# The expert stage of a decoder layer as dense matmuls over both whole tables, in place of row fetches

## The chip, the cores and the metric

The kernel runs on one core of one Trainium2 chip. The metric is the device time of one execution in microseconds; the median of three runs of the kernel before is 2040.55 us (2039.8 to 2042.72).

## The reference

One layer of a decoder, on 512 prompt tokens and 32 sample tokens (8 sequences of 4), D = 1024, everything in f32. First a mixer: RMSNorm, one input projection, a gMLP part and an attention part with three dilated windows (12 heads of 64; the samples attend to a cache of keys and values), then an output projection added to x. Then the expert part ("PEER"), which this case is about:

```python
def block(xb):                                    # xb: RMSNorm of x, tokens x 1024
    q = (xb @ w_q).reshape(TOK_BLK, PEER_HEADS, 2, DK_HALF)          # 8 heads, 2 halves of 128
    s = jnp.einsum('thcd,hcnd->thcn', q, sub_keys)                   # 128 scores for each half
    s1, i1 = lax.top_k(s[:, :, 0], TOPK)                             # the best 16 of each half
    s2, i2 = lax.top_k(s[:, :, 1], TOPK)
    cand = s1[..., :, None] + s2[..., None, :]                       # 16 x 16 sums
    cid = i1[..., :, None] * N_KEYS + i2[..., None, :]               # expert number, 0 to 16383
    top_s, pos = lax.top_k(cand, TOPK)
    eid = take_along_axis(cid, pos)
    g = softmax(top_s)
    hid = gelu(einsum('thkd,td->thk', u_tab[eid], xb))
    return einsum('thk,thkd->td', g * hid, v_tab[eid])
```

So each token selects 8 x 16 = 128 of 16384 experts. Each expert has a row of 1024 in `u_tab` and one in `v_tab`, 67.1 MB a table. The result is added to x, and a last RMSNorm gives y. The gates and the hidden values are per token and expert; the sum over a token's 128 experts is all that leaves the stage.

## The kernel before

Tokens lie in five tiles: four of 128 prompt tokens and one of the 32 samples (`TILES`, lines 39 to 41). The program is written out engine by engine: each of `block.sync`, `block.tensor`, `block.scalar`, `block.vector` and `block.gpsimd` is one list of instructions that runs in order, and semaphores tie the lists together. A wait therefore holds back all that stands behind it in its list.

**Up to the expert stage** (lines 317 to 604; to about 354 us). Norm and transposes, the input projection (`L474`, stationary: 128 columns of the normed x, moving: 384 or 512 columns of weights), attention (`L506` to `L564`; for the samples three pairs of heads work side by side in column strips of 32, `L517`), and the output projection (`project_out`, `L593`; the sample tile in strips, `L598`).

**Scoring.** For each head and tile, `queries` (`L622`) multiplies 128 tokens (stationary) with 256 columns of w_q (moving), `turn_queries` transposes the result, and `key_scores` (`L641`) gives 2 x 128 scores. ScalarE copies each result out of PSUM (`copy`, `L718`).

**Routing.** `route` (`L1112` to `L1167`) finds, on VectorE, the 16 best of each half, the 256 sums, the 16 best of these, and from their positions the expert numbers (one-hot compare `L1152`, product `L1156`, sum `L1160`, then two instructions that make the number and write it to `eid`). It is a chain of 13 links, each waiting for the one before. `finish_gates` makes the softmax.

**The experts.** A step is one head of one tile: 16 slots. For each slot, GpSimd fetches, by an indirect DMA (`L1339`), one row of `u_tab` for each of 128 tokens: 128 x 4 KB. `dots` (`L1223`) multiplies them with x on VectorE and sums. ScalarE takes the Gelu (`L870`), VectorE multiplies with the gates (`weights`, `L1229`), ScalarE makes for each slot a diagonal matrix of the 128 weights (`L877`), and `slot` (`L651`) multiplies it with the 128 fetched rows of `v_tab`, two matmuls of 512 columns, adding into one PSUM sum of the tile. The 32 samples are spread over 128 partitions, four slots at a time, so their eight heads take two steps. That makes 34 steps x 16 = 544 slots. The rings hold 8 rows blocks for `u_tab` and 4 for `v_tab` (`UR`, `VR`, line 64). Routing of the next tile's heads is spread over the steps of the tile before. The end is `copy` of the sum, a square, a root and `finish_y` (`L1207`).

Of the kernel before, what the change touches and what calls it, by code (L numbers as in the profile page):

```python
# [14 lines left out]
P = 128  # L28
# [35 lines left out]
UR, VR = 8, 4  # L64


GROUPS = P // NSAMP
LINKS = 13
STEPS = [HEADS] * (NT - 1) + [HEADS // GROUPS]
FIRST = [sum(STEPS[:t]) for t in range(NT)]  # L70
NSTEP = sum(STEPS)


def build(nc, x_p, x_s, k_cache, v_cache, gains, w_in, ln_gb, w_sT, b_sT, w_out, w_q, keysT, u_tab, v_tab,
          ident_c, logc_c, smask_c, snew_c, rope_c, iota_c, tril_c, blockm_c,
          y_p, y_s, k_p, v_p, k_s, v_s, gv_s):
    ctx = ExitStack()
    with ctx:
# [8 lines left out]
        area_w = sb("area_w", 16384)  # L87
        area_r = sb("area_r", 14720)
        area_t = sb("area_t", KD * TOK)
        area_x = sb("area_x", NT * D)  # L90
        area_v = sb("area_v", 6400)
# [22 lines left out]
        u_ring = [cut(area_r, s * D, D) for s in range(UR)]  # L114
        v_ring = [cut(area_r, (UR + s) * D, D) for s in range(VR)]
        keys = cut(area_r, (UR + VR) * D, 2 * HEADS * NKEYS)
# [15 lines left out]
        h_stage = [cut(area_v, s * D, D) for s in range(2)]  # L132
        v_tok = cut(area_v, 0, NT, DB)
        u_tok = cut(area_v, NT * DB, NT, DA)
        vn = cut(area_v, NT * (DB + DA), NT, DA)
        xn = cut(area_v, 0, NT, D)
# [16 lines left out]
        iota = sb("iota", TOPK)  # L153
# [4 lines left out]

        eid = sb("eid", NSTEP * TOPK, U32)
        gate = sb("gate", NSTEP * TOPK)  # L160
        hid = sb("hid", TOPK)
        gelu = sb("gelu", TOPK)
        wts = sb("wts", TOPK)
        ident4 = sb("ident4", NSAMP)

        diag = [cut(area_c, s * P, P) for s in range(VR)]
        q_row = cut(area_c, 512, 2 * P)
        q_col = cut(area_c, 768, 2, P)
        s_cur = [cut(area_v, NT * D + a, 2, NKEYS) for a in (0, 1024)]
        s_left = cut(area_v, NT * D + 256, 2, NKEYS)  # L170
        cand = cut(area_c, 1024, TOPK * TOPK)
        cand_left = cut(area_c, 1280, TOPK * TOPK)
        hot = [cut(area_v, NT * D + 512 + c * 256, TOPK, TOPK) for c in range(2)]
        tops = cut(area_c, 1536, HEADS, TOPK)
        eid_samp = cut(area_c, 1664, SLOTS)
        gate_samp = cut(area_c, 1792, SLOTS)
        rt = cut(area_c, 1920, 9 * TOPK)
        rtu = sb("rtu", 5 * TOPK, U32)
        val = [rt[:, c * TOPK:(c + 1) * TOPK] for c in range(2)]
        idf = [rt[:, (2 + c) * TOPK:(3 + c) * TOPK] for c in range(2)]  # L180
        pick = [rt[:, (4 + c) * TOPK:(5 + c) * TOPK] for c in range(2)]
        top = rt[:, 6 * TOPK:7 * TOPK]
        den8 = rt[:, 7 * TOPK:7 * TOPK + 8]
        rden8 = rt[:, 7 * TOPK + 8:8 * TOPK]
        eidf = rt[:, 8 * TOPK:9 * TOPK]
        idx = [rtu[:, c * TOPK:(c + 1) * TOPK] for c in range(2)]
        pos = rtu[:, 2 * TOPK:3 * TOPK]
        digit = [rtu[:, (3 + c) * TOPK:(4 + c) * TOPK] for c in range(2)]

# [8 lines left out]
        acc = bank[0]  # L198
        x_cur = wide(1, D)
        ps_q, ps_qT, ps_s = half(4), half(5), half(6)  # L200
# [24 lines left out]
        q_done, q_copied, q_turned, qT_copied = sem("q_done"), sem("q_copied"), sem("q_turned"), sem("qT_copied")  # L225
        s_done, s_ready = sem("s_done"), sem("s_ready")
        tops_exped = sem("tops_exped")
        u_landed = [sem(f"u_landed{s}") for s in range(UR)]
        v_landed = [sem(f"v_landed{s}") for s in range(VR)]
        u_free, v_free = sem("u_free"), sem("v_free")  # L230
# [7 lines left out]
        block = ctx.enter_context(nc.Block())  # L238


        N_CONST = 1 + NT + 1 + 2 * NB + 7 + GROUPS
# [1186 lines left out]
```

## Time and profile before

| | |
|---|---|
| median of three runs | 2040.55 us |
| profiled execution, its own time | 2051.2 us |
| its span, first to last instruction | 2048.3 us |
| mean granted TensorE clock | 0.966 of full speed |
| instructions | 19348 |

The profile is of one execution. Busy times are those of instructions that compute; waiting and DMA-issuing instructions are not in them, save that GpSimd's indirect DMAs are (their work on GpSimd is real). The 40 slices of the page are 51.2 us each. PE is TensorE, PEld its weight loads (beside the matmuls), DVE VectorE, ACT ScalarE, POOL GpSimd, SP SyncE, which has the plain loads. In names, `area_w`, `area_r` and so on are pieces of on-chip memory that are used for many things in turn, and `bank` is PSUM.

### The profile page before, as it was taken

The page shows a single profiled execution, that of the slowest core. Times are in us where ns is not written, and L with a number is a line of the kernel's source. Part 1 is how long each engine was busy: PE and PEld are TensorE (multiplying, and loading weights), DVE is VectorE, ACT ScalarE, POOL GpSimd, SP SyncE. Part 2 cuts the span into 40 slices and gives each one's busy share as a digit, 9 for nine tenths or more (in the row PEclk, how much of TensorE's full clock was granted, in tenths as well). Part 3 has the DMA queues.
Part 4 walks back from the last instruction along what each step waited for, and adds up shares of the span by engine and source line. Part 5 has one row for each costly group of instructions (what it writes and reads, how often), then busy time and mean ns, then how long its engine had stood idle before and what let it go on. Part 6 is the DMA issues. An engine that isn't in the chain of part 4 may idle for free.

```text
span 2048.3 us, 19348 instructions
## 1 busy us (share of the span) xinstructions
PE 1625.9 (79%) x5414; PEld 745.2 (36%) x5414; DVE 1147.9 (56%) x3207; ACT 392.8 (19%) x1051; POOL 1057.8 (52%) x1168
## 2 busy tenths in 40 slices
PE   6999888978888877777777778777777777877677
PEld 3566454444443333333333333333322323322211
DVE  2220565467677777656555665666556555666641
ACT  2111443122221111111111211111121111111212
POOL 3000100145565565566666666666666666666663
PEclk9999899999999999999999999999999999999999
DMA  6110875588998898899999999999999999999996
GB/s 214 63 66 9 305 264 190 203 312 309 322 345 335 335 332 336 324 362 369 371 353 358 369 376 368 354 363 367 364 361 374 352 366 367 357 359 358 380 367 240
DMA packets 188136, 640.99 MB, mean 313 GB/s; under 512 B 19408, under 2 KB 35072, under 8 KB 187936
## 3 DMA queue, kind: packets, MB, share of 16 engines
q0 software_dynamic: 160640, 587.53, 77.0%
q1 hardware_dynamic: 27424, 52.60, 7.5%
q8 instruction: 34, 0.56, 0.1%
q14 instruction: 38, 0.31, 0.0%
HBM read 634.44 MB, written 5.60 MB: 312 GB/s over the span
## 4 chain that ended last, share of the span: by engine, by line
PE 34%; DMA 19%; POOL 16%; DVE 13%; issue 12%; another core or an unknown queue 3%; ACT 1%; DVEq 0%; SPq 0%; ACTq 0%; POOLq 0%
POOL area_r L1339 16%; PE bank L651 13%; DMA area_r<-in_v_tab,eid 11%; PE bank L474 8%; DMA area_r<-in_u_tab,eid 7%; PE bank L622 4%; DVE area_r L1223 4%; PE bank L593 3%; PE bank L564 1%; PE bank L412 1%; PE bank L517 1%; DMA area_w<-in_w_in 1%; PE bank L471 1%; DMA area_w<-in_v_cache 1%
## 5 line engine op out<-in xcount | busy, mean ns | idle before, releaser
L651 PE MATMUL bank<-area_r,area_c 128*128 128x512 f32 (+1 forms) x2176 | 1067.6, 623 | 348.8 <-DMA area_r<-in_v_tab,eid 282.6
L1223 DVE CUSTOM_DVE_ANT_0 area_r<-area_r,bank 128x1024 f32<-128x1024 f32 x544 | 640.4, 1218 | 308.5 <-DMA area_r<-in_u_tab,eid 284.8
L651 PEld LDWEIGHTS bank<-area_r,area_c 128*128 128x128 f32 (+1 forms) x2176 | 380.7, 190 | 965.7 <-issue 838.9
L1339 POOL DMA_INDIRECT area_r<-in_v_tab,eid x544 | 514.9, 947 | 399.8 <-PE bank L651 199.5
L1339 POOL DMA_INDIRECT area_r<-in_u_tab,eid x544 | 510.4, 938 | 288.3 <-issue 156.6
L877 ACT ACTIVATE area_c<-ident,wts 128x128 f32<-128x128 f32 (+1 forms) x544 | 197.5, 391 | 557.8 <-PE bank L651 266.4
L474 PE MATMUL bank<-area_w,area_t 128*128 128x384 f32 (+1 forms) x448 | 158.7, 510 | 7.5 <-DMA area_w<-in_w_in 5.9
L622 PE MATMUL bank<-area_w,area_t 128*128 128x256 f32 (+3 forms) x640 | 145.7, 381 | 3.2 <-ACT area_c L718 2.5
L622 PEld LDWEIGHTS bank<-area_w,area_t 128*128 128x128 f32 (+1 forms) x640 | 110.8, 175 | 47.0 <-issue 19.8
L474 PEld LDWEIGHTS bank<-area_w,area_t 128*128 128x128 f32 x448 | 84.4, 192 | 70.0 <-issue 17.5
L1317 POOL MEMSET area_x<- 128x192 f32 x2 | 0.5, 258 | 151.6 <-ACT area_r L718 151.6
L718 ACT ACTIVATE area_v<-bank 128x256 f32<-128x256 f32 (+3 forms) x54 | 20.8, 385 | 268.4 <-remote 96.9
L718 ACT ACTIVATE area_c<-bank 128x256 f32<-128x256 f32 (+1 forms) x80 | 28.8, 360 | 222.5 <-remote 157.8
L718 ACT ACTIVATE area_x<-bank 128x384 f32<-128x384 f32 (+7 forms) x97 | 38.4, 422 | 152.8 <-PE bank L474 76.6
L1035 DVE CUSTOM_DVE_ANT_0 area_x<-bank,area_c 96x640 f32<-96x640 f32 (+4 forms) x64 | 29.1, 492 | 66.6 <-PE bank L506 51.1
L1334 POOL DMA_DIRECT2D area_w<-in_v_cache x8 | 7.0, 879 | 106.6 <-DMA area_w<-in_k_cache 56.2
L593 PE MATMUL bank<-area_w,area_t 128*128 128x512 f32 x128 | 55.3, 593 | 1.2 <-issue 1.2
L870 ACT ACTIVATE gelu<-hid 128x16 f32<-128x16 f32 x34 | 7.3, 215 | 242.6 <-issue 191.7
L1134 DVE MAX8 area_c<-area_c 128x8 f32<-128x256 f32 (+1 forms) x40 | 17.0, 426 | 61.3 <-remote 44.0
L996 DVE TENSOR_TENSOR rope_ab<-area_x,rope 128x96 f32<-128x96 f32 (+1 forms) x20 | 5.1, 256 | 79.3 <-ACT area_x L718 79.3
L1223 DVE DVE_READ_ACCUMULATOR2_ANT hid<- 128x1 f32 x544 | 44.8, 82 | 0.0
L1138 DVE MATCH_VALUE_LOAD rtu<-area_c 128x8 f32 (+1 forms) x40 | 3.6, 90 | 71.0 <-remote 59.7
(136 smaller groups left out, 1058.9 us busy)
## 6 DMA issues: line engine op xcount, KB each, us to landing
area_w<-in_k_cache SPq DMA_DIRECT2D x8, 1920.0 KB, 9.2
area_w<-in_v_cache POOLq DMA_DIRECT2D x8, 1920.0 KB, 9.1
area_w<-in_w_in SPq DMA_DIRECT2D x6, 1536.0 KB, 12.6
area_r<-in_u_tab,eid POOLq DMA_INDIRECT x544
area_r<-in_v_tab,eid POOLq DMA_INDIRECT x544
area_w<-in_w_q SPq DMA_DIRECT2D x8, 1024.0 KB, 10.6
area_x<-in_x_p SPq DMA_DIRECT2D x8, 512.0 KB, 8.9
area_w<-in_w_out SPq DMA_DIRECT2D x1, 4096.0 KB, 14.0
```

The lines of the kernel that those rows point to most:

```text
L412: return pe.transpose(out, src, ident[0:n, 0:n])
L471: mm = pe.matmul(half(u % 3)[CG * g:CG * g + n, 0:m], featT[:, k, a:a + n], w_ring[c % W_SLOTS][:, k, g * m:(g + 1) * m], start=(k == 0), ...
L474: mm = pe.matmul(half(u % 3)[0:n, 0:w], featT[:, k, a:a + n], w_ring[c % W_SLOTS][:, k, 0:w], start=(k == 0), stop=(k == KD - 1))
L517: mm = pe.matmul(wide(u % 2, D)[CG * g:CG * g + CG, lo:hi], q_blk[b % 2][:, pr * CG:(pr + 1) * CG], src[:, pr, :], start=(i == 0), stop=(i ...
L593: mm = pe.matmul(half(c)[0:n, :], featT[:, k, a:a + n], w_o[:, k, c * 512:(c + 1) * 512], start=(k == 0), stop=(k == KD - 1))
L622: mm = pe.matmul(ps_q[0:n, 0:2 * P], featT[:, k, a:a + n], area_w[:, bass.ds(h * WQ + k * 2 * P, 2 * P)], start=(k == 0), stop=(k == KD - 1))
L651: mm = pe.matmul(acc[0:n, c, :], diag[s][:, 0:n], v_ring[s][:, c * 512:(c + 1) * 512], start=False, stop=False, skip_group_check=True)
L718: return nc.scalar.activation(out, src, ACT.Copy, scale=scale)
L877: nc.scalar.activation(diag[j % VR][:, 0:n], eye[:, 0:n], ACT.Copy, scale=wts[:, j:j + 1]).then_inc(diag_ready, 1)
L1035: return vec.tensor_tensor_reduce(out=out, in0=scores, in1=counts, scale=-1.0, scalar=3e38, op0=ALU.add, op1=ALU.min, accum_out=least)
L1223: vec.tensor_tensor_reduce(out=u_ring[s], in0=u_ring[s], in1=x_cur, scale=1.0, scalar=0.0, op0=ALU.mult, op1=ALU.add, accum_out=hid[:, j:j ...
L1339: nc.gpsimd.indirect_dma_start(out=ring[s], out_offset=None, in_=table, in_offset=bass.IndirectOffsetOnAxis(ap=eid[:, column:column + 1], ...
```

## The change

The experts are no longer fetched. The tokens are taken in two groups: 256 (tiles 0 and 1), and 288 (tiles 2 and 3 and the samples). An expert's number is 128 i1 + i2. A step handles the 128 experts with one i2 (all i1); 2 x 128 = 256 steps.

- **Table one** (`table_one`): a block of `u_tab`, transposed on the host, 512 KB, is loaded by SyncE into a ring of four. Eight matmuls, stationary 128 x 128 of the block, moving 256 or 288 tokens of x, give 128 experts x tokens. ScalarE takes the Gelu into a ring of 58 blocks (`mix`); the samples have one of 24.
- **The weight matrix**: for each token, 128 x 128 (i1 by i2), zero where an expert isn't selected. `route` now keeps i1 and i2 apart (12 links, no number made), and writes them and the gates to `slots`. `turn_slots` transposes these, so that a token's 128 slots lie along partitions. For a token, `hots` makes on VectorE two matrices, slots x 128: gate at i1, and 1 at i2. `build_weights` multiplies the two; four tokens (a quad) fill one bank, and ScalarE copies it in strides into a stage of 32 tokens. GpSimd's queue writes each stage of 2 MB to memory (`w_kept`), and SyncE loads it back by blocks of eight i2 (`load_w_block`).
- `mixes` multiplies the Gelu block with the weights of that i2 on VectorE.
- **Table two** (`table_two`): stationary 128 experts x 128 tokens of the mixed block, moving 512 columns of the block of `v_tab`; four matmuls a step, adding in four banks through all 128 steps. For the samples, every fourth step, 8 matmuls with 32 columns of weights, each of four steps in its own strip of 32 partitions of a bank; the four strips are added at the end.
- **Queries** now hold w_q stationary and move 256 or 288 tokens, so their result needs no transpose; the key scores of the second group go to memory (`s_kept`) and are loaded again for its routes. x goes to memory (`x_kept`) while its place holds the stages, and is loaded back.
- Order: 16 heads of scores, then the steps. Routes of the first two tiles stand before the steps, the other 24 between steps 57 and 103; table two of group 0 begins at step 57 and goes in up to two a step; the last 18 of group 1 stand behind the last step. All loops are written out.

The diff, cut to its core:

```diff
+G1 = G2 = 256
+STEPS = 2 * N2
+RING, SRING = 58, 24
+UR, VR = 4, 6
+QUAD = 4
+CHUNK = 32
+BLOCK = 8
+V_FROM = 57
+LAG = 18
+def quads_upto(step):
+    return upto(0, 64, 4, 52, step) if step < 75 else upto(64, QUADS - 64, 75, 131, step)
+SLOTS_AT = {0: 2, 1: 3, 2: 74, 3: 98, 4: 122}
...
 # sync
+            for s in range(STEPS + 1):
+                if s == V_FROM - 8:
+                    sp.wait_ge(route_link, 2 * HEADS * LINKS)
+                    for v in range(VR):
+                        load_v(v)
+                    for b in range(2):
+                        sp.wait_ge(s_stored[b], 16 * HEADS)
+                        sp.wait_ge(w_stored[b], 16 * stored_before(G1 // CHUNK)[b])
+                    load_w_block(0)
+                    load_w_block(1)
+                if s + UR < STEPS:
+                    sp.wait_ge(h_done, s + 1)
+                    load_u(s + UR)
+                for v in v_in(s):
+                    if v + VR < STEPS:
+                        what, value = v_free_for(v + VR)
+                        if what == "tiles":
+                            sp.wait_ge(v_done, value)
+                        else:
+                            sp.wait_ge(samp_done, value)
+                        load_v(v + VR)
...
 # tensor
+            def table_one(s):
+                g, _ = group_of(s)
+                a, n = first_token(g), width(g)
+                pe.wait_ge(u_landed[s % UR], 16 * (s // UR + 1))
+                if s >= 2:
+                    pe.wait_ge(h_read, s - 1)
                 for k in range(KD):
+                    mm = pe.matmul(half(6 + s % 2)[:, 0:n], u_ring[s % UR][:, k, :], featT[:, k, a:a + n],
                                    start=(k == 0), stop=(k == KD - 1))
+                mm.then_inc(h_done, 1)
+            def build_weights(q):
+                pe.wait_ge(hot_ready, q + 1)
+                if q >= 1:
+                    pe.wait_ge(w_copied, q)
+                for i in range(QUAD):
+                    mm = pe.matmul(ps_w[:, i * P:(i + 1) * P], hot[q % 2][0][:, i, :], hot[q % 2][1][:, i, :],
+                                   start=True, stop=True)
+                mm.then_inc(w_built, 1)
+            def table_two(v):
+                g, i2 = group_of(v)
+                pe.wait_ge(mixed, v + 1)
+                pe.wait_ge(v_landed[v % VR], 16 * (v // VR + 1))
+                if g == 1 and i2 == 0:
+                    pe.wait_ge(acc_read, 4)
+                for j in range(2):
+                    for c in range(2):
+                        mm = pe.matmul(half(2 * j + c), mix[v % RING][:, j * P:(j + 1) * P],
+                                       v_ring[v % VR][:, c * 512:(c + 1) * 512], start=(i2 == 0), stop=(i2 == N2 - 1))
+                mm.then_inc(v_done, 1)
+                if g == 1 and i2 % 4 == 3:
...
+                    for c in range(2):
+                        for r in range(4):
+                            mm = pe.matmul(half(4 + c)[r * NSAMP:(r + 1) * NSAMP, :], mix_samp[(v - N2 - 3 + r) % SRING],
+                                           v_ring[(v - 3 + r) % VR][:, c * 512:(c + 1) * 512],
+                                           start=(i2 == 3), stop=(i2 == N2 - 1))
+                    mm.then_inc(samp_done, 1)
...
+            for i in range(2, 2 * HEADS):
+                queries(i)
+                key_scores(i - 1)
+            key_scores(2 * HEADS - 1)
+            pe.wait_ge(s_copied, 2 * HEADS)
+            for s in range(STEPS + 1):
+                if s < STEPS:
+                    table_one(s)
+                for t in range(NT):
+                    if SLOTS_AT[t] == s:
+                        turn_slots(t)
+                for q in quads_in(s):
+                    build_weights(q)
+                for v in v_in(s):
+                    table_two(v)
...
 # scalar
+            def copy_weights(q):
...
+                copy(w_stage[c % 2][:, :, j * QUAD:(j + 1) * QUAD],
+                     ps_w.rearrange("p (t i) -> p i t", t=QUAD)).then_inc(w_copied, 1)
...
 # vector
+            def hots(q):
...
+                for i in range(QUAD):
+                    vec.tensor_scalar(hot[q % 2][0][:, i, :], iota[:], st[:, 0, j + i:j + i + 1], st[:, 2, j + i:j + i + 1],
+                                      ALU.is_equal, ALU.mult)
+                vec.tensor_tensor(hot[q % 2][1], iota[:].unsqueeze(1).to_broadcast([P, QUAD, P]),
+                                  st[:, 1, j:j + QUAD].unsqueeze(2).to_broadcast([P, QUAD, P]),
+                                  ALU.is_equal).then_inc(hot_ready, 1)
...
+            for k in range(2 * HEADS):
+                route(k)
+            finish_gates(0)
+            finish_gates(1)
+            for s in range(STEPS + 1):
+                for v in v_in(s + 2):
+                    mixes(v)
+                for q in quads_in(s + 1):
+                    hots(q)
+                for k in routed_in(s):
+                    route(k)
...
 # gpsimd
-            for i in range(TOPK):
-                gather_u(i)
-            for i in range(NSTEP * TOPK):
-                if i + TOPK < NSTEP * TOPK:
-                    gather_u(i + TOPK)
-                gather_v(i)
```

## Rows read from the trace of the kernel before

**Rows 1.** The page, the span in 40 slices: DMA engines, busy tenths.
```profile
DMA  6110875588998898899999999999999999999996
```

**Rows 2.** The page, DMA queues: packets, MB, share of 16 engines.
```profile
q0 software_dynamic: 160640, 587.53, 77.0%
...
HBM read 634.44 MB, written 5.60 MB: 312 GB/s over the span
```

**Rows 3.** The page, the chain that ended last, shares of the span by line.
```profile
POOL area_r L1339 16%; PE bank L651 13%; DMA area_r<-in_v_tab,eid 11%; PE bank L474 8%; DMA area_r<-in_u_tab,eid 7%; PE bank L622 4%; DVE area_r L1223 4%; PE bank L593 3%; PE bank L564 1%; PE bank L412 1%; PE bank L517 1%; DMA area_w<-in_w_in 1%; PE bank L471 1%; DMA area_w<-in_v_cache 1%
```

**Rows 4.** Busy time by stretch: PE, PEld, DVE, ACT, POOL, granted clock, DMA share, GB/s.
```profile
1000.00:1500.00 500.00, 381.52 (x924) 164.71 (x922) 304.98 (x775) 81.87 (x227) 327.50 (x347) 0.98 0.97 363
```

**Rows 5.** The page, costliest groups: busy us, mean ns, idle before.
```profile
L651 PE MATMUL bank<-area_r,area_c 128*128 128x512 f32 (+1 forms) x2176 | 1067.6, 623 | 348.8 <-DMA area_r<-in_v_tab,eid 282.6
L1223 DVE CUSTOM_DVE_ANT_0 area_r<-area_r,bank 128x1024 f32<-128x1024 f32 x544 | 640.4, 1218 | 308.5 <-DMA area_r<-in_u_tab,eid 284.8
```

**Rows 6.** The page, DMA issues: KB each, us to landing.
```profile
area_w<-in_k_cache SPq DMA_DIRECT2D x8, 1920.0 KB, 9.2
```

**Rows 7.** The chain in order of time, 370 to 428 us: start, us, what.
```profile
375.89 0.61 ACT area_t L718
...
376.63 0.64 PE bank L412 x4
...
383.89 3.47 PE bank L622 x16
...
389.66 34.34 PE bank L593 x80
423.99 2.73 PE bank L598 x34
...
427.16 0.46 issue
```

**Rows 8.** Busy time by stretch, for the granted clock (third from the end).
```profile
50.00:200.00 150.00, 150.00 (x756) 92.07 (x755) 28.32 (x116) 23.57 (x62) 1.20 (x6) 1.00 0.14 47
...
389.66:424.00 34.34, 34.34 (x83) 14.93 (x85) 29.81 (x84) 3.27 (x7) 15.73 (x17) 1.00 0.66 232
...
300.00:350.00 50.00, 43.01 (x404) 25.10 (x401) 28.48 (x116) 19.06 (x57) 2.50 (x6) 0.87 0.56 203
```

**Rows 9.** TensorE's instructions in order of time, at 339 and 388 us.
```profile
339.66 2.35 PE L517 MATMUL bank<-area_w,area_x 128*32 128x512 f32 x24
...
388.95 0.71 PE L641 MATMUL bank<-area_r,area_c 128*128 128x128 f32 x4 [0.47 <-ACT area_c L718]
```

**Rows 10.** VectorE's instructions in order of time: a route's first, and what follows it.
```profile
517.32 0.48 DVE L1119 MAX8 area_c<-area_v 128x8 f32<-128x128 f32 x2
...
527.67 1.22 DVE L1223 CUSTOM_DVE_ANT_0 area_r<-area_r,bank 128x1024 f32<-128x1024 f32 x1
```

**Rows 11.** Groups by line and shape, VectorE.
```profile
L1156 DVE TENSOR_TENSOR area_v<-area_v,area_c 128x256 f32<-128x256 f32 x64 | 24.5, 424 | 5.1 <-DVE area_v L1152 0.5
...
L1126 DVE MAX8 area_c<-area_v 128x8 f32<-128x128 f32 x64 | 15.6, 286 | 5.0 <-DVE area_v L1123 0.5
...
L1134 DVE MAX8 area_c<-area_c 128x8 f32<-128x256 f32 x32 | 13.7, 428 | 42.7 <-remote 26.0 <-issue 13.5 <-DVE rtu L1132 0.9
...
L1051 DVE TENSOR_SCALAR area_x<-area_x,att 128x128 f32<-128x128 f32 x12 | 3.4, 287 | 0.4
```

**Rows 12.** Groups by line and shape, ScalarE.
```profile
L718 ACT ACTIVATE area_c<-bank 128x256 f32<-128x256 f32 x64 | 24.1, 377 | 175.6 <-remote 111.5 <-PE bank L412 36.8 <-PE bank L622 21.1
...
L718 ACT ACTIVATE area_t<-bank 128x512 f32<-128x512 f32 x16 | 9.1, 596 | 53.2 <-PE bank L412 46.2 <-issue 6.8
...
L799 ACT ACTIVATE area_x<-area_x,att 128x256 f32<-128x256 f32 x12 | 6.0, 500 | 5.3 <-DVE att L1035 5.3
```

**Rows 13.** The chain in order of time, the last 13 us.
```profile
2035.30 5.33 PE bank L651 x12
...
2044.66 1.27 DVE area_x L1207
```

More of the change, by code:

```diff
@@ L171, in build @@
[L171 to L177, printed above, removed]
+        ident4 = sb("ident4", NSAMP)
+        slots = [sb("slots0", 3 * SLOTS)[:].rearrange("p (a s) -> p a s", a=3), cut(area_x, 9728, 3, SLOTS)]
@@ L196, in wide @@
             return bank[i].rearrange("p a b -> p (a b)")[:, 0:n]
-        acc = bank[0]
-        x_cur = wide(1, D)
-        ps_q, ps_qT, ps_s = half(4), half(5), half(6)
+        ps_w, ps_slots = half(4), half(5)
         x_in = [sem(f"x_in{t}") for t in range(NT)]
@@ L614, in turn_xn, with queries @@
                 mm.then_inc(xn_turned, 1)
-            def queries(t, h, n_done):
-                a, n = TILES[t]
-                if not isinstance(n_done, int) or n_done:
-                    pe.wait_ge(q_copied, n_done)
+            def queries(i):
+                g, h = i // HEADS, i % HEADS
+                a, n = first_token(g), width(g)
+                if i >= 2:
+                    pe.wait_ge(q_copied, i - 1)
+                if i == 0:
+                    pe.wait_ge(xnT_ready, 4)
+                if i == HEADS:
+                    pe.wait_ge(xnT_ready, 2 * NT)
+                if g == 0:
+                    pe.wait_ge(wq_in[h], 16)
+                for c in range(2):
+                    for k in range(KD):
+                        mm = pe.matmul(bank[(i + 1) % 2][:, c, 0:n], wq[h][:, k, c * P:(c + 1) * P], featT[:, k, a:a + n],
+                                       start=(k == 0), stop=(k == KD - 1))
+                mm.then_inc(q_done, 1)
@@ new lines, in key_scores @@
+            def key_scores(i):
+                g, h = i // HEADS, i % HEADS
+                pe.wait_ge(q_copied, i + 1)
+                if i >= 2:
+                    pe.wait_ge(s_copied, i - 1)
+                if i == 0:
+                    pe.wait_ge(keys_in, 16)
+                for j in range(2 if g == 0 else 3):
+                    n = P if j < 2 else NSAMP
+                    for c in range(2):
+                        out = (half(4 + i % 2)[:, j * WIDE + c * NKEYS:j * WIDE + (c + 1) * NKEYS] if j < 2
+                               else half(6 + i % 2)[0:n, c * NKEYS:(c + 1) * NKEYS])
+                        mm = pe.matmul(out, q_col[i % 2][:, c, j * P:j * P + n],
+                                       keys[:, (2 * h + c) * NKEYS:(2 * h + c + 1) * NKEYS], start=True, stop=True)
+                mm.then_inc(s_done, 1)
@@ L928, in _ @@
+            act.wait_ge(samp_done, N2 // 4)
+            copy(samp_sum, bank[2].rearrange("p a b -> p (a b)")).then_inc(samp_copied, 1)
+            for t in range(2, NT):
+                square_y(t)
         @block.vector
@@ L1293, in _ @@
+            for t in range(2, NT):
+                add_sums(t)
+            for t in range(2, NT):
+                finish_y(t)
         @block.gpsimd
@@ L1335, in _ @@
                     vc_in[b % 2], 16)
-            def gather(ring, s, table, column, landed):
-                nc.gpsimd.indirect_dma_start(
-                    out=ring[s], out_offset=None, in_=table,
-                    in_offset=bass.IndirectOffsetOnAxis(ap=eid[:, column:column + 1], axis=0)).then_inc(landed[s], 16)
-            def gather_u(i):
-                if i % TOPK == 0:
-                    pool.wait_ge(eid_ready, i // TOPK + 1)
-                pool.wait_ge(u_free, i + 1)
-                gather(u_ring, i % UR, u_tab, i, u_landed)
```

696 lines of the change are left out of this document (346 added, 350 removed).

## The prediction

> **What bounds the kernel now.** I read the page from the top. The DMA row is at 9 tenths from about 400 us to the end [rows 1], and nearly all bytes are in one queue, the row fetches [rows 2]. That fits the code: 544 columns x 2 tables x 128 rows x 4 KB = 570 MB, of 634 MB read. The chain of waits gives its largest shares to issuing the fetches on GpSimd, to their landing and to the matmuls that eat the rows [rows 3]. The table by stage says it plainest: from 1000 to 1500 us the DMA engines are 0.97 busy at 363 GB/s, TensorE 382 of 500 us [rows 4]; the groups of instructions show TensorE and VectorE both waiting on landings, 282.6 and 284.8 us [rows 5]. So the expert stage, which runs from the jump in the ninth slice of rows 1 (410 to 460 us) to the end, is bound by transfer: 570 MB / 363 GB/s = 1571 us of some 1600. But TensorE is far from free: its slack there is only about a quarter.
>
> **What the change removes.** All 1088 row fetches, 544 dot products (1218 + 82 ns each, 685 us of VectorE), 544 diagonal copies and 1088 matmuls of 512 columns. DMA is relieved: each of two token groups streams both tables, 2 x 2 x 67.1 = 268 MB, and the weight matrix goes out and back (17 x 2.1 MB, twice, 71 MB). With 4 MB for x this is some 345 MB in over 2000 us, 170 GB/s, half of what the rows above carry. Block loads of like size landed at 1.9 MB in 9.2 us [rows 6], 209 GB/s; two 512 KB blocks in a step of 7 us are 150 GB/s. Transfers stop being the bound.
>
> **What it adds on TensorE.** The arithmetic is now over all 16384 experts. First the price of a column. Two instructions are issued for each f32 matmul (64 matmuls in L593, 128 instructions). Eighty of 512 columns took 34.34 us, 429 ns each; sixteen of 256 columns 3.47 us, 216 ns each; between them there is no gap [rows 7]. So a matmul costs 0.858 us per 512 columns, weight loads hidden. The granted clock was 1.00 in those stretches [rows 8], 2.4 GHz, its higher level: nothing cheaper is to be had.
> - Table one, group 0: 128 steps x 8 matmuls x 256 columns = 3.45 us a step. Group 1 has 288 columns: 3.45 x 288/256 = 3.88 us. 442 + 497 = 939 us.
> - Table two: 256 steps x 4 matmuls x 512 columns = 3.43 us a step, 879 us.
> - The 32 samples: 8 matmuls (32 columns wide) of 512 columns at every fourth of 128 steps, four of them in the four column strips of one bank. One after the other they would be 256 x 0.858 = 220 us; in full concurrency 55 us. Nearest row: L517, 24 instructions of 512 or 128 columns in three strips took 2.35 us [rows 9]; one by one 12 x 0.429 + 12 x 0.107 = 6.4 us, so 2.7 of three strips were had. I take 62 us and keep 55 and 220.
> - Weight matrix: 136 quads x 4 matmuls of 128 columns. Below: 8 x 0.107 = 0.86 us a quad (117 us); above: four such instructions in 0.71 us [rows 9], 1.42 us (193 us). That short row includes the drain of its last, so I take the lower side, 0.96 us, 131 us.
>
> Against the strips speaks the Trainium skill, "TensorEngine Tiling (Array Packing)", Key Properties: changing the tiling mode drains the engine; and "TensorE: Matmul & The Clock Gate", Part 3, has 2.38 times for three strips. By the latter an estimate of the sample work is 220/2.38 = 92 us if the fourth strip gives nothing, and my sum would be 30 us more. As to the drain, the trace doesn't bear it out here: the 32-wide L598 starts at 423.99, where the 128-wide L593 ends at 424.00 [rows 7].
>
> **The start of the stage.** Up to 354.58 us nothing that counts is moved. Then on TensorE: eight halves of the output projection, 8 x 6.87 = 55 us; two sample halves at 3.2 us (the first took that; in the second TensorE waited for nothing shown, in "issue" gaps [rows 7], which I count as bad luck) 6.5; ten groups of transposes, each followed by an ACT copy, 10; queries, now with the weights stationary, 8 x 6.9 + 8 x 7.76 = 117; key scores 19; waits 3. That is 565 us, and three steps of table one end at 575. Step 2 then turns tile 0's slots, which needs all 16 routes of the first two tiles. Head 0 is scored at about 438 us; a route took 10.35 us, 517.32 to 527.67, where the next work starts [rows 10], and loses its last two links, 0.65 us: 9.7. So 16 x 9.7 = 155 us, to 594, and exponentials, a table load of 1.28 us, gates and turn make 598. VectorE is slower than TensorE here, and TensorE stands still for about 23 us.
>
> **What lies beside.** VectorE per quad: four products of 128 elements at 287 ns and one of 512, 424 + 2 x 142 = 708 ns (the 424 of L1156 at 256 elements, and for 256 more twice what MAX8 takes more at 256 than at 128, 428 - 286) [rows 11]: 1.86 us; per table-two step one product of 256, 424 ns. In steps 75 to 103, the densest, that is 9.7/2 + 1.6 x 0.43 + 1.3 x 1.86 = 8.0 us a step against TensorE's 3.45 + 1.6 x 3.43 + 1.3 x 0.96 = 10.2. ACT: a Gelu of 256 out of PSUM lies between 377 (copy) and 500 ns (Exp with sum) [rows 12]; a weight copy of 512 took 596 ns in a contiguous shape; under 2 us a step. All hidden. What isn't: one bank holds a quad, so a step with two quads has TensorE wait for the copy, about 0.75 us (a copy of 0.61, and transposes 0.74 after its start [rows 7]; I count 0.8); written in strides it may be twice that. 32 such steps: 26 us, up to 45. And at step 49 SyncE waits for chunk 7 of the matrix, which is built in step 51: table-one blocks stand behind it, then behind two 1 MB weight blocks. The ring holds four steps, so TensorE waits some 8 us about step 53. In group 1 SyncE stands behind the sample sums for up to three steps; the four blocks already there cover that.
>
> **Sum.** 598 (restart at step 2, with three steps of table one done) + 125 x 3.45 = 431 + 497 + 879 + 62 + 131 + 26 + 8 + small waits 10 + end 11 (from the last matmul 7.7 us today, 2040.6 to 2048.3 [rows 13], plus the sample sum's copy, two matmuls and more tiles to finish) = 2653 us of span. The profiled run takes 2051.2 beside a span of 2048.3, so 2656; it lies 0.5% above the median of 2040.55. Waiting on TensorE rather than fetches I expect less of that: 2655 us. With every low bound at once (no start stall, 55, 117, no waits) it is 2565; with the high ones for strips, quads and copies 2892.
>
> **The rivals.**
> 1. Four strips don't run side by side, because here each has its own moving rows as well. L517 shares none either, which speaks against it. +158 us: 2815. Chance 0.06.
> 2. Quads and routes lock. Hot vectors are double-buffered, builds wait for copies, and a route of 9.7 us sits in VectorE's queue between them; if each of the 24 late routes costs TensorE 3 us and each quad 0.3: +72 +41, 2765. The 2.2 us of slack per step speaks against. 0.15.
> 3. The small waits pull the granted clock down. In 300 to 350 us, where TensorE idles in short pieces, the clock is 0.87 [rows 8]. Were it 0.87 in steps 4 to 51 and 75 to 130, some 807 us, the price is 807 x (1/0.87 - 1) = 120 us: 2775. Beside it stands the Trainium skill's "TensorE: Matmul & The Clock Gate", A second HAM failure mode: frequent micro-idling between groups lets the clock oscillate. Against: from 1000 to 1500 us, with more idling than I expect here, it was 0.98. 0.05.
> 4. Not slower: the transfer bound was the price and dense work hides under it. It decides at TensorE's price for the two tables: they may cost at most 1818 - 610 = 1208 us, two thirds of the rate above, as if both instructions of a matmul ran partly side by side the way strips do. The total would be 2045. Against: 80 instructions in a row with no such overlap. 0.02.
> The forecast has 0.72: 2653 with its own spread, 2600 to 2720.
>
> **Range and chances.** 2590 to 2790 takes in rivals 2 and 3 and most of the bounds, leaving rival 1 and the ends out. A difference under 0.2% can't be told from none. Faster 0.01, same 0.01, slower 0.98.
>
> **What would show it.** TensorE over 95% busy from 600 us on, at clock 1.00; DMA half busy, near 170 GB/s; L-lines of table one and two at 216 to 242 and 429 ns an instruction; one gap of some 20 us at about 575; sample matmuls adding under 2 us at every fourth step; VectorE at about 60%. It would be wrong if a table-one step took much off 3.45 us, or if TensorE waited for VectorE or landings by hundreds of us.

## The result and the profile after

The changed kernel takes 2635.75 us (median of 4 runs, 2630.49 to 2637.2) against 2040.17 (the three runs of before and one more): 1.293 times the kernel before, 95% interval 1.288 to 1.297. The forecast was 2655, range 2590 to 2790. The profiled execution has a span of 2628.7 us; the sum had 2653.

The page of the changed kernel, engines' totals and slices, against [rows 1]; its queues, against [rows 2]; and its chain by line, against [rows 3]:

```profile
PE 2535.0 (96%) x10773; PEld 1637.0 (62%) x10773; DVE 799.2 (30%) x2894; ACT 353.4 (13%) x902; POOL 65.6 (2%) x142
...
PE   7998899999997999999999999999999999999998
...
DMA  5107662025556555555555556333344443333343
...
q1 hardware_dynamic: 137104, 358.95, 40.0%
q0 software_dynamic: 8960, 59.69, 6.2%
...
HBM read 372.75 MB, written 45.84 MB: 159 GB/s over the span
...
PE bank L745 35%; PE bank L767 33%; PE bank L552 6%; PE bank L755 5%; PE bank L709 5%; PE bank L776 2%; PE bank L671 2%; PE bank L642 1%; PE bank L490 1%; ACT area_x L827 1%; PE bank L725 1%; PE bank L595 1%; DMA area_w<-in_w_in 1%; PE bank L549 1%; DMA area_w<-in_v_cache 1%
```

Fewer bytes, DMA half idle, TensorE 96% busy, and 68% of the chain in the two tables: L745 is table one, L767 table two, L755 the builds, L776 the samples. By stretch, columns as in [rows 4]: the steps with one-hot products, then plain steps of group 1.

```profile
850.00:1560.00 710.00, 698.32 (x2600) 451.16 (x2599) 326.88 (x1170) 77.62 (x152) 14.90 (x28) 1.00 0.56 182
1560.00:2000.00 440.00, 439.22 (x1560) 266.55 (x1559) 34.19 (x126) 35.00 (x128) 3.13 (x6) 1.00 0.44 157
```

The granted clock is 1.00, the 2.4 GHz level. TensorE's instructions in order of time show the price of a step:

```profile
1962.18 3.60 PE L767 MATMUL bank<-area_r,area_w 128*128 128x512 f32 x8
1965.71 1.92 PE L776 MATMUL bank<-area_r,area_x 128*32 128x512 f32 x16
1967.56 4.15 PE L745 MATMUL bank<-area_t,area_r 128*128 128x288 f32 x16
1971.55 3.60 PE L767 MATMUL bank<-area_r,area_w 128*128 128x512 f32 x8
1974.98 4.04 PE L745 MATMUL bank<-area_t,area_r 128*128 128x288 f32 x16
1978.86 3.60 PE L767 MATMUL bank<-area_r,area_w 128*128 128x512 f32 x8
```

Read the starts, not the durations, which overlap: table two 3.43 us (1971.55 to 1974.98), table one 3.88, samples 1.85. These are the prediction's 3.43 and 3.88 from [rows 7]. And the start of the stage, where a gap of 23 us was forecast (L490 here are the slots being turned):

```profile
562.45 10.63 PE L745 MATMUL bank<-area_t,area_r 128*128 128x256 f32 x48 [0.94 <-ACT area_r L827]
572.92 0.49 PE L490 MATMUL bank<-ident,slots 128*128 128x128 f32 x3
573.24 3.62 PE L745 MATMUL bank<-area_t,area_r 128*128 128x256 f32 x16
...
589.18 1.05 PE L755 MATMUL bank<-area_w 128*128 128x128 f32 x8
591.01 1.13 PE L755 MATMUL bank<-area_w 128*128 128x128 f32 x8 [0.78 <-ACT area_x L827]
591.98 3.62 PE L745 MATMUL bank<-area_t,area_r 128*128 128x256 f32 x16
...
834.30 16.02 PE L745 MATMUL bank<-area_t,area_r 128*128 128x256 f32 x66 [14.49 <-DMA area_r<-in_u_tabT]
```

There is none: the last route ends at 565.7 us, and the slots are turned at 572.92 without a wait. The two waits that do count are for the weight copy (0.78 us, 32 times) and one of 14.49 us for a table-one block.

Of the other signs named ahead, DMA was 0.49 busy at 168 GB/s and TensorE 98% busy from 600 us on, as said. VectorE is a miss: about 60% was forecast, and it is 30% busy, 46% in the stretch with routes and products.

### The profile page after: what moved, and what is told of

Read it like the earlier page. It is cut to its first block, busy times and chain, and to the rows that moved or that the text cites. A ratio compares the mean times of both kernels' runs of the same rounds, so it can differ in the third digit from the quotient of the medians.

```text
span 2628.7 us, 27616 instructions
## 1 busy us (share of the span) xinstructions
PE 2535.0 (96%) x10773; PEld 1637.0 (62%) x10773; DVE 799.2 (30%) x2894; ACT 353.4 (13%) x902; POOL 65.6 (2%) x142
## 4 chain that ended last, share of the span: by engine, by line
PE 94%; DMA 2%; issue 2%; DVE 1%; ACT 1%; SPq 0%; POOL 0%; ACTq 0%; POOLq 0%; DVEq 0%
PE bank L745 35%; PE bank L767 33%; PE bank L552 6%; PE bank L755 5%; PE bank L709 5%; PE bank L776 2%; PE bank L671 2%; PE bank L642 1%; PE bank L490 1%; ACT area_x L827 1%; PE bank L725 1%; PE bank L595 1%; DMA area_w<-in_w_in 1%; PE bank L549 1%; DMA area_w<-in_v_cache 1%
## 5 line engine op out<-in xcount | busy, mean ns | idle before, releaser
L745 PE MATMUL bank<-area_t,area_r 128*128 128x256 f32 (+1 forms) x4096 | 983.8, 394 | 15.4 <-DMA area_r<-in_u_tabT 14.5
L745 PEld LDWEIGHTS bank<-area_t,area_r 128*128 128x128 f32 x4096 | 773.1, 190 | 260.9 <-issue 103.5
L767 PE MATMUL bank<-area_r,area_w 128*128 128x512 f32 x2048 | 912.2, 592 | 0.0
L767 PEld LDWEIGHTS bank<-area_r,area_w 128*128 128x128 f32 x2048 | 384.4, 190 | 410.8 <-issue 395.6
L1321 DVE TENSOR_TENSOR area_w<-area_w,area_r 128x256 f32<-128x256 f32 x256 | 102.4, 420 | 943.8 <-DMA area_r<-w_kept 943.0
L1309 DVE TENSOR_SCALAR area_w<-iota,area_x 128x128 f32<-128x128 f32 x544 | 151.6, 343 | 415.5 <-PE bank L755 411.3
L755 PE MATMUL bank<-area_w 128*128 128x128 f32 x1088 | 145.9, 277 | 24.9 <-ACT area_x L827 24.9
L827 ACT ACTIVATE area_x<-bank 128x512 f32<-128x512 f32 (+5 forms) x248 | 123.3, 507 | 318.5 <-PE bank L552 113.7
L755 PEld LDWEIGHTS bank<-area_w 128*128 128x128 f32 x1088 | 140.0, 191 | 35.5 <-issue 30.1
L709 PE MATMUL bank<-area_t,area_w 128*128 128x256 f32 (+1 forms) x512 | 122.5, 398 | 0.0
L490 PE MATMUL bank<-ident,area_x 128*128 128x128 f32 (+2 forms) x292 | 46.6, 289 | 17.0 <-DVE area_x L1065 10.4
L776 PE MATMUL bank<-area_r,area_x 128*32 128x512 f32 x512 | 61.6, 598 | 0.0
L490 PEld LDWEIGHTS bank<-ident,area_x 128*128 128x128 f32 (+2 forms) x292 | 33.7, 148 | 40.0 <-issue 27.4
L776 PEld LDWEIGHTS bank<-area_r,area_x 128*32 128x32 f32 x512 | 13.3, 109 | 43.4 <-issue 43.4
```

The source lines that it names most:

```text
L490: return pe.transpose(out, src, ident[0:n, 0:n])
L709: mm = pe.matmul(bank[(i + 1) % 2][:, c, 0:n], wq[h][:, k, c * P:(c + 1) * P], featT[:, k, a:a + n], start=(k == 0), stop=(k == KD - 1))
L745: mm = pe.matmul(half(6 + s % 2)[:, 0:n], u_ring[s % UR][:, k, :], featT[:, k, a:a + n], start=(k == 0), stop=(k == KD - 1))
L755: mm = pe.matmul(ps_w[:, i * P:(i + 1) * P], hot[q % 2][0][:, i, :], hot[q % 2][1][:, i, :], start=True, stop=True)
L767: mm = pe.matmul(half(2 * j + c), mix[v % RING][:, j * P:(j + 1) * P], v_ring[v % VR][:, c * 512:(c + 1) * 512], start=(i2 == 0), stop=(i2 ...
L776: mm = pe.matmul(half(4 + c)[r * NSAMP:(r + 1) * NSAMP, :], mix_samp[(v - N2 - 3 + r) % SRING], v_ring[(v - 3 + r) % VR][:, c * 512:(c + 1 ...
```

## Experiments

What differs by chance lies ahead of the expert stage. The changed kernel run again has a span of 2633.4 us in place of 2628.7, but it also reaches the stage later:

```profile
567.23 10.63 PE L745 MATMUL bank<-area_t,area_r 128*128 128x256 f32 x48 [0.94 <-ACT area_r L827]
```

From the first matmul of table one (562.45 us, here 567.23) to the end both have 2066.2 us. The start varies from 556.25 to 567.65 us over the f32 runs below; why isn't shown. So the length of the stage is compared, in us, each of one profiled execution:

| kernel | span | stage | against 2066.2 |
|---|---|---|---|
| 1, half of table one | 2162.8 | 1606.6 | -459.7 |
| 2, no streaming | 2615.1 | 2049.9 | -16.3 |
| 3, one strip | 2794.8 | 2231.5 | +165.3 |
| 4, links apart | 2653.7 | 2086.0 | +19.8 |
| 5, two banks | 2592.7 | 2031.8 | -34.5 |
| 6, blocks spread | 2574.8 | 2018.4 | -47.9 |
| 7, wide samples | 2676.5 | 2110.6 | +44.4 |
| 9, queues alone | 2634.8 | 2067.9 | +1.7 |

Kernels 1, 2 and 7 leave out part of the result, as each expectation says; the others compute all of it.

**1. Half of table one.** `for k in range(KD)` becomes `for k in range(KD // 2)` in `table_one` (and the `stop` with it).

> The changed kernel with four of the eight matmuls of each table-one step (half of the model dimension is left out of the hidden values); all loads, builds, products and waits stay. Theory, columns on TensorE set the time: each of 256 steps loses 4 matmuls, 1.73 us in group 0 and 1.94 us in group 1, 128 x 1.73 + 128 x 1.94 = 470 us; the span falls from 2628.7 to about 2160, less what appears behind it. Rival A, table-two or the transfers are the true pace: under 100 us gained. Rival B, VectorE is close behind in steps 4 to 51 (2.5 us of products a step against 3.46 / 2 + 1.2) and 75 to 103 (8 us against 8.4): some 30 to 60 us of the 470 don't come, 2190 to 2220, and TensorE shows waits for the one-hot products.

The span is 466 us less, 460 of them in the stage, of 470. Columns on TensorE are the pace, at nearly their full price, even where VectorE was thought close. TensorE never waits for a one-hot product; it waits 2.7 us for slots, and the table-one stall is 2 us longer. Rivals A and B fall.

**2. No streaming.** In the steps, `load_u` and `load_v` are left out, and TensorE waits for the first load of a slot only.

```diff
                     sp.wait_ge(h_done, s + 1)
-                    load_u(s + UR)
...
-                        load_v(v + VR)
```

> The changed kernel, but only the first four blocks of the first table and the first six of the second are ever loaded; every later step uses what lies in the rings (so all experts but a few are left out of the result). Instructions on TensorE, ScalarE and VectorE are the same. Theory, the transfers are hidden under TensorE: 502 loads of 512 KB fewer, DMA share in the steady steps from 0.44 to under 0.1, and the span stays within 20 us of 2628.7; only the 14.5 us stall at 834 us for a table-one block can go, so about 2612. Rival, TensorE is slowed by transfers (contention in on-chip memory, late blocks that the chain hides): 50 us or more gained, with fewer ns per instruction.

TensorE's groups of this kernel, busy us and mean ns of one:

```profile
L765 PE MATMUL bank<-area_r,area_w 128*128 128x512 f32 x2048 | 912.2, 592 | 0.0
L743 PE MATMUL bank<-area_t,area_r 128*128 128x288 f32 x2048 | 520.0, 407 | 0.0
```

The changed kernel's own two lines read 912.2 and 520.0 as well. With 263 MB less read, no matmul is quicker. (The DMA share from 850 to 1500 us is 0.13, from 2000 on 0.06; under 0.1 was expected.) The transfers cost the 16.3 us by which the stage is shorter, and that is the one stall: from the end of step 52 to the start of step 53 TensorE loses 14.6 us, and another 1.6 behind it, where 80 instructions take 18.88 us (834.30 to 853.18) that cost 17.28 elsewhere. The granted clock (third from the end of the row) had fallen while TensorE stood still:

```profile
834.30:850.00 15.70, 15.70 (x66) 13.61 (x67) 14.98 (x57) 1.23 (x4) 1.08 (x2) 0.90 0.57 197
```

**3. One strip for the samples.** `half(4 + c)[r * NSAMP:(r + 1) * NSAMP, :]` becomes `half(4 + c)[0:NSAMP, :]`, adding up through `r`.

> The changed kernel with the samples' matmuls of all four steps writing the same strip of 32 partitions, adding up there, in place of a strip each. Same count of instructions and columns. Theory, the four strips run side by side and that saves what the prediction took from the rows of attention: 16 instructions of 512 columns now need 16 x 0.215 = 3.44 us per group of four and bank pair x 2 = 6.87 us a group in place of 1.85, so +5.0 x 32 = +160 us, 2790. Rival, the strips gain little, the cost was hidden elsewhere: under +50 us.

The stage is 165.3 us longer. The same 16 instructions:

```profile
2008.70 7.05 PE L776 MATMUL bank<-area_r,area_x 128*32 128x512 f32 x16
2015.69 4.15 PE L745 MATMUL bank<-area_t,area_r 128*128 128x288 f32 x16
```

6.99 us where the four strips take 1.85, and 32 times the difference is 164 us: 3.8 of 4 are had. Rival 1's price (+158) was about right and its case doesn't occur.

**4. A semaphore instruction behind each link of a route.**

```diff
                     dve.wait_ge(route_link, k * LINKS + done[0])
+                    dve.sem_inc(passed, 1)
```

> The changed kernel with the semaphore instruction put back that the kernel before has behind each of a route's waits on VectorE (12 in a route). A route took 10.35 us before and takes 8.25 us now, where the prediction had 9.7. Theory, that instruction is the difference, about 0.12 us a link: a route goes to about 9.7 us, 16 routes end 23 us later, TensorE waits for them at step 2 of the experts, and the span is 15 to 25 us longer, about 2650. Rival, the routes were slower before because of GpSimd's fetches beside them: the route stays at 8.3 us and the time within 3 us of the changed kernel's.

Median of 4 runs 2651.32 (+15.6); the span is 25.0 us longer, but 5.2 of these come before the stage, which is 19.8 longer. VectorE, the last instruction of a route and the first of the next:

```profile
536.38 0.69 DVE L1289 TENSOR_REDUCE area_x<-area_x 128x32 f32<-128x512 f32 x1
537.21 0.49 DVE L1260 MAX8 area_c<-area_r 128x8 f32<-128x128 f32 x2
...
546.80 0.49 DVE L1260 MAX8 area_c<-area_r 128x8 f32<-128x128 f32 x2
```

A route is 9.59 us, 1.34 more (0.11 a link); in the changed kernel MAX8 starts at 532.72 and 540.97, 8.25 us. And a gap as forecast is there:

```profile
596.26 0.90 PE L491 MATMUL bank<-ident,slots 128*128 128x128 f32 x3 [17.98 <-DVE slots L1296]
```

**5. Two banks for the quads, a later wait for the weight blocks.**

```diff
-                if s == V_FROM - 8:
+                if s == V_FROM - 5:
...
-        ps_w, ps_slots = half(4), half(5)
+        ps_w, ps_slots = [half(4), half(5)], half(5)
...
-                if q >= 1:
-                    pe.wait_ge(w_copied, q)
+                if q >= 2:
+                    pe.wait_ge(w_copied, q - 1)
...
```

Two more waits guard the bank that slots and quads then share.

> The changed kernel with two small repairs: SyncE asks for the first weight blocks at step 52 in place of 49, so that the loads of table one for steps 53 on no longer stand behind the wait for chunk 7; and the quads alternate between two banks, so that TensorE doesn't wait for the copy when a step has two. Theory: both waits are on the path, since TensorE is 96% busy and nothing else is near: 14.5 us at step 53 and 24.9 us (32 x 0.78) go, and nothing takes their place, span 2628.7 - 39 = 2589, time about 2596. Rival: one-hot products of VectorE, which are double-buffered against the builds, are next in steps 4 to 51; then only the 14.5 us come, 2614.

Median of 4 runs 2598.39; the stage is 34.5 us shorter. The copy waits are gone: two builds in a row take 1.79 us with what follows them, where they took 2.80 (589.18 to 591.98), so each wait cost 1.01, not 0.78, and 32 of them 32 us. The rival falls. But the stall didn't go, it moved from step 53 to step 56:

```profile
823.56 9.15 PE L753 MATMUL bank<-area_t,area_r 128*128 128x256 f32 x32 [11.15 <-DMA area_r<-in_u_tabT]
```

SyncE's own waits for the store of the last weight chunk say why (the first two lines are of the changed kernel, the third of this one; `w_kept<-area_x` is the store):

```profile
SPq L454 <- DMA w_kept<-area_x: 22.6, 1, 22.6
824.69 1.00 SPq L435 DMA_DIRECT2D area_r<-w_kept  x2
...
SPq L460 <- DMA w_kept<-area_x: 12.9, 1, 12.9
```

In the changed kernel SyncE stands in that wait for 22.6 us, until 824.69; the table-one load for step 53 stands behind it, is issued at 825.74, and TensorE goes on at 834.30. With the wait at step 52 it is the same again, three steps later. The chunk is built in step 51 and its store issued at 799.52; SyncE is let go only at 813.30, while TensorE had run out of blocks at 812.4. The store took 13.8 us here and 7.4 in the changed kernel; 3 MB of table two had been asked for just before it.

**6. The blocks spread out** (from 5: one block of the second table a step from step 45, weight blocks at 52 and 54, each behind the step's load of table one).

> The kernel with two banks, with the first six blocks of the second table asked for one a step from step 45, the first weight block at step 52 behind that step's load of table one, the second at step 54. With only the wait moved, the stall before step 57 was still 11.2 us (14.5 before). Theory, what delays the load of table one is not the wait but 5 MB of other blocks ahead of it (6 x 0.5 + 2 x 1 MB, some 16 us at 310 GB/s): spread out, the stall goes, span 2592.7 - 11 = 2582. Rival, the stall is that of the first weight block itself: it stays at 5 us or more, or moves to the products on VectorE.

Median 2577.88 (2576.61 to 2579.31). TensorE waits for no table block at all, and the stage is 13.4 us shorter than in 5: the wait of 11.15 and some 2 us of slower matmuls behind it. SyncE's wait for the store is down from 12.9 to 4.8 us. The theory above set the 5 MB against the wait, and that isn't shown: three things changed at once (the spreading, the order of the loads, the later second weight block), and in 5 the late load had stood behind the wait.

**7. Samples full width.** Four 128-wide matmuls in place of eight 32-wide ones.

> The changed kernel with the samples' 8 narrow matmuls of each fourth step replaced by 4 full-width ones of 512 columns into the same banks (the samples' sum is then not theirs: their expert part is left out), so that TensorE never changes between full width and strips of 32 in the steps. By columns, a group of four steps needs 4 x 0.858 = 3.43 us in place of the strips' 1.85: +1.58 x 32 = +51 us. Theory, each change of width costs about 0.1 us on either side (a table-one step after strips starts its successor 3.99 us later, in place of 3.88, and strips start 3.53 after table two in place of 3.43): 64 x 0.1 = 6.7 us go as well, and the trace shows 3.43 and 3.88 everywhere, +44 us, 2673. Rival, the 0.1 us are not the width's: they stay, +51 us.

The span is 47.8 us longer, the stage 44.4, as the theory has it. The starts say the same:

```profile
2009.35 3.60 PE L767 MATMUL bank<-area_r,area_w 128*128 128x512 f32 x8
2012.78 3.60 PE L776 MATMUL bank<-area_r,area_w 128*128 128x512 f32 x8
2016.22 4.04 PE L745 MATMUL bank<-area_t,area_r 128*128 128x288 f32 x16
2020.10 3.60 PE L767 MATMUL bank<-area_r,area_w 128*128 128x512 f32 x8
```

3.43, 3.44, 3.88, where the changed kernel has 3.53 before its strips and 3.99 behind. A change of width costs 0.10 us, 64 of them 6.7 us.

**8. bf16 operands.** GpSimd's queue casts the tables while loading (into bf16 views of the rings); x, the mixed values and the one-hot matrices are written as bf16; sums, queries, scores and routes stay f32.

```diff
-                mm = pe.matmul(half(6 + s % 2)[:, 0:n], u_ring[s % UR][:, k, :], featT[:, k, a:a + n],
+                mm = pe.matmul(half(6 + s % 2)[:, 0:n], u16[s % UR][:, k, :], x16[k][:, a:a + n],
```

> The changed kernel with bf16 operands in the expert matmuls (tables, x, mixed hidden values, one-hot matrices; sums stay f32, and so do queries, scores and routes): GpSimd's queue loads the tables and casts them on the way, SyncE's queue takes over the stores and score loads. Theory: an f32 matmul costs four times its columns at 2.4 GHz (0.858 us for 512), a bf16 one once; the two tables fall from 1818 to about 455 us of TensorE, the builds from 121 to 31. Then the transfers are next, 345 MB in the expert stage at 340 to 360 GB/s, about 1000 us, and VectorE in steps 4 to 131 (24 routes x 8.25 + 136 quads x 1.9 + products 56 = 510 us). From step 2 at 573 us: 120 + 430 + 440 + 15, total about 1590, faster than both kernels. Rival A: loads that cast run slower than plain ones (half the rate: about 2000 us). Rival B: TensorE's rate does not depend on the type, total 2630.

1615.42 us (4 runs, 1614.61 to 1618.87), 0.853 of the kernel before (0.849 to 0.856): the one version that beats both, though with less precise products. Its page, TensorE at one step, and two stretches:

```profile
L742 PE MATMUL bank<-area_r 128*128 128x256 bf16 (+1 forms) x1792 | 308.3, 323 | 191.5 <-DMA area_r<-in_u_tabT 185.1
L764 PE MATMUL bank<-area_r,area_w 128*128 128x512 bf16 x1024 | 317.0, 447 | 40.8 <-DMA area_r<-in_v_tab 30.2
...
1306.62 1.02 PE L742 MATMUL bank<-area_r 128*128 128x288 bf16 x7
1307.48 0.29 PE L742 MATMUL bank<-area_c,area_r 128*128 128x288 bf16 x1
...
800.00:900.00 100.00, 53.70 (x276) 30.40 (x277) 96.09 (x356) 17.46 (x36) 21.84 (x39) 0.74 0.80 170
1150.00:1600.00 450.00, 320.09 (x1754) 161.69 (x1755) 62.57 (x264) 62.35 (x250) 148.13 (x264) 0.86 0.96 194
```

There is one instruction a matmul (1024 for table two, where f32 had 2048), and seven of 288 columns start within 0.86 us, 0.123 each, a quarter of f32's 0.485. TensorE waits for landings, and from 1150 us on DMA is 0.96 busy: transfer binds again there. It isn't the only bound: from 800 to 1000 us, where the late routes are, VectorE is 0.96 and 0.94 busy and DMA 0.80 to 0.85, and TensorE waits 91.6 us in all for one-hot products. (GB/s there counts what arrives, 256 KB an issue, half of what a table block has in memory.) Rival B falls, and A too: the forecast at full rate was 1590.

**9. The queues alone.** As 8, in f32.

> The changed kernel in f32, with only the queues exchanged as in the bf16 kernel: GpSimd loads the tables, SyncE stores and loads the rest. The bf16 kernel changed the type and the queues at once. Theory, the 1000 us that it gained are the type's: here the TensorE instructions keep 216 and 429 ns and the span stays within 20 us of 2628.7. Rival, the queue of the loads matters: 50 us or more to either side.

The stage is 1.7 us longer. In f32 the queue is worth nothing; the 1000 us are the type's.

**10. 8 with the repairs of 5 and 6.**

> The kernel with bf16 operands, with two banks for the quads and the first blocks of the second table and of the weights spread over steps 45 to 54. In the bf16 kernel's steps the DMA engines were 0.93 to 1.05 busy and VectorE 0.95 from 800 to 1000 us; TensorE waited 185 us for table one and 92 us for one-hot products. Theory, the transfers bind there, so what these repairs gave TensorE in f32 (39 us and 15 us) mostly doesn't come: time within 25 us of 1615 where the kernel before takes 1893; where that takes 2050 (363 in place of 397 GB/s in its stage), the transfers of some 900 us cost 9% more, about 1615 + 80 = 1695. Ratio to the kernel before 0.82 to 0.86 in either case. Rival, TensorE's waits for copies and blocks are on the path as in f32: 40 us faster, 1575 (or 1655).

1625.08 us (1616.11 to 1631.85), where the kernel before takes 1896.96; ratio 0.856 (0.854 to 0.859). As expected nothing came: TensorE still waits 176.9 us for table one and 109.8 for one-hot products. Repairs that gave 48 us of the stage in f32 are worth that only where TensorE is the bound. How the bf16 kernel does on a chip with slow fetches wasn't tried.

**11. The kernel before again.**

> The kernel before, unchanged, for its profile on this chip. It took 1896.7 us on the chip of the last four runs and 2040.2 on the one before, while the changed kernel's TensorE times are the same to 0.1%. Theory: its transfers are faster there: the same 587 MB in the queue of row fetches, at 1000 to 1500 us over 363 GB/s by the ratio of the stage's lengths, (1600 / 1456) x 363 = 399 GB/s. Rival: the DMA rate is the same and something else (a wait, the clock) differs.

The span is 1893.7 us. The stretch of [rows 4]:

```profile
1000.00:1500.00 500.00, 413.05 (x1022) 175.25 (x1021) 335.00 (x857) 96.72 (x250) 354.22 (x377) 0.99 1.01 397
```

397 GB/s, not 363, for the same fetches, with the DMA engines as busy as before (1.01 and 0.97).

**12. The changed kernel again.**

> The changed kernel itself, on the chip of this job. The kernel before took 2040 us on one chip and 1893 to 1897 on two others, where its stage of fetches moved 397 GB/s in place of 363. Theory, the changed kernel is bound by TensorE's columns, which cost the same everywhere: 2630 to 2645 us, and the ratio follows the kernel before, 1.29 where that is slow and 1.39 where it is fast. Rival, the changed kernel gains from faster transfers as well: under 2600 us where the kernel before takes 1895.

2637.63 us (2635.22 to 2638.3), on a chip where the kernel before takes 2052.62 (7 runs): ratio 1.285, 1.281 to 1.289. So the changed kernel itself was never run where the kernel before is fast. The kernels of 4 and 5 were, beside a kernel before of 1897 and 1893 us, and stand at 1.397 and 1.372 times it. Their stages, and those of 1 to 3 on the same chip as 4, differ from 2066.2 us by what their own edits account for (to 1 us in 2 to 5, to some 5 us in 1). That bears the theory out and leaves the rival little room. Over the five sessions, the last four on four different chips, the kernel before took 2040, 1897, 1893, 2053 and 1897 us.

## Why the prediction was right, and where it was off

- **The bound moves from transfer to TensorE, at 0.858 us per 512 columns.** Right, and shown from both sides by experiments 1 and 2. Rows of another stage with the same instruction ([rows 7]) gave the steps of both tables to 0.01 us, and 1818 us for all.
- **The start.** The step that failed is "a route ... 9.7 us ... VectorE is slower than TensorE here, and TensorE stands still for about 23 us". A route takes 8.25 us; 16 end 23 us earlier; TensorE goes on with table one at 573.2 us, not 598. I had taken off the two lost links and overlooked that the change also drops an instruction behind every wait (`wait_apart` becomes a bare wait). Experiment 4 puts it back: 9.59 us a route, 1.34 of the 1.45 that I was off, and an 18 us gap. This is the whole of the 24 us that the sum was too long. That the errors below add up to nearly nothing is luck:
- **Builds** 0.89 us a quad (580.48 to 581.37 and after), not 0.96: 121, not 131.
- **Samples** 1.85 us a group, 59 of 62 us; experiment 3. The changes of width, which I took as free because two modelled times met in [rows 7], cost 6.7. By the Trainium skill, "TensorEngine Tiling (Array Packing)", Key Properties, changing the tiling mode drains the engine; it gives no price, and the trace agrees that a change costs something, 0.10 us each here. The Trainium skill's 2.38 times for three strips ("TensorE: Matmul & The Clock Gate", Part 3) would, by the estimate in the prediction, have made it 30 us more; it isn't met here: four strips do 3.8 times the work of one.
- **Copy waits** 32 us, 1.01 each, not 26.
- **The stall for table one** 16 us with the slow matmuls behind it, not 8, but at the step and from the cause that were forecast: SyncE's wait for the chunk built in step 51 (experiment 5). The prediction didn't count the store of that chunk, 7.4 us from its issue to SyncE's release.
- **Small waits** 10 us in the sum; 2 are left of them.
- **End** 10.9 us after the last sample matmul, 11 forecast.
- Sum: 573.2 + 432 + 497 + 879 + 59 + 7 + 121 + 32 + 16 + 11 = 2627, of 2628.7.
- **Rivals.** Strips: experiment 3. Routes and quads locking: TensorE never waits for a one-hot product, and what the quads cost are the copy waits. The clock: 1.00 from 575 to 825 and from 850 to 2000 us, in the very steps where 0.87 was feared; between these it fell, while TensorE stood in the one long stall (0.64, and 0.90 in the 16 us behind it). Not slower: the tables cost 1818 us, not 1208, and experiment 1 has their columns at nearly full price.
- **VectorE at about 60%** doesn't follow from the prediction's own terms: 24 routes, 136 quads and 256 products at its prices are some 600 us of a stage of 2055, 29%. Measured are 26%.
- I counted the 0.5% by which the profile lay above the median as a trait of the fetches. The changed kernel's profiled execution lies 0.2% below its median, within the spread of its four runs. That brought the forecast 5 us closer to the median by luck.

## What to carry to other kernels

Turning fetches into dense work is a trade of bytes for columns: multiply both out with rows of the same kernel before writing it. Here 570 MB became some 345, and 1088 f32 matmuls of 512 columns, 933 us at 0.858, became 1818 us. An f32 matmul took four times what a bf16 one did (0.485 and 0.123 us for 288 columns); with bf16 operands the same plan wins. And when a step is moved or rewritten, count the wait and semaphore instructions too: they are in no busy time, but twelve a route made a gap of 18 us. And before a stall is put down to the load that ended it, read what the queue that issued the load was waiting for.

## What the runs showed of the hardware

- The kernel bound by fetches varies by 8% between sessions on different chips (1893 to 2053 us), with 397 or 363 GB/s in the same stretch of two profiles (for the 363 it isn't on record which chip it was); whether the chip itself makes the difference, or what ran beside the core, isn't shown. The f32 kernel bound by TensorE has 2636 and 2638 us. A ratio of two kernels with different bounds holds for the session it was taken in: 1.29 here; beside a kernel before of 1895 us, 2637 would be 1.39 (worked out, not run).
- Loads that cast f32 to bf16 took as much of the 16 DMA engines as plain ones, though half as much arrived. The queue of experiment 9 read 321 MB in f32, 35.5% of 2634.8 us, 935 us. The same queue with the same 86912 packets, casting, has 56.6% of 1617.0 us in experiment 8, 915 us (on another chip).
- TensorE's small waits: a wait of 0.78 us in the trace costs 1.01 us from start to start (experiment 5); why isn't shown.
- A stall of TensorE costs more than its gap: after 14.5 us of standing still the granted clock was 0.90 over the next 15.7 us, and 80 matmul instructions took 1.6 us more than elsewhere.
- In f32 the expert stage repeats closely: 2066.2 us in two profiled executions whose spans differ by 4.7.
